# Seven weight slots, three natural expert pairs and one wide ordered pair in the middle of a two-layer backbone step

## The reference

```
def hier_moe(h, w_group, b_group, w_expert, b_expert, w_gate, w_up, w_down):
    ...
    g_prob = jax.nn.softmax(xf @ w_group + b_group, axis=-1)
    p_grp, g_idx = lax.top_k(g_prob, 1)
    ...
    e_w, e_idx = lax.top_k(jax.nn.softmax(e_logit, axis=-1), TOP_K_INNER)
    ...
    act = jax.nn.silu(jnp.einsum('td,edf->tef', x, w_gate)) * jnp.einsum('td,edf->tef', x, w_up)
    act = act * combine[..., None]
    y = jnp.einsum('tef,efd->td', act, w_down)
```

## Time and profile before

| | us |
|---|---|
| median of 3 timed runs | 1143.74 (1143.3 to 1143.93) |
| profiled execution | 1141.77 |
| its span | 1139.6 |
| PE busy | 981.8 (86%) |
| VectorE busy | 291.4 (26%) |
| ScalarE busy | 195.5 (17%) |
| GpSimd busy | 24.8 (2%) |

### The profile page before, as it was taken

How to read it: one execution, slowest core, us unless ns; L and a number is a source line. 1 busy time by engine, 2 the same in 40 slices (tenths; PEclk the granted TensorE clock), 3 DMA queues, 4 the chain that set the end, 5 groups by cost and what they waited for, 6 DMA issues and landing times.

```text
span 1139.6 us, 13423 instructions
## 1 busy us (share of the span) xinstructions
PE 981.8 (86%) x5665; PEld 528.6 (46%) x5665; DVE 291.4 (26%) x644; ACT 195.5 (17%) x348; POOL 24.8 (2%) x45
## 2 busy tenths in 40 slices
PE   3799999989899786886699999999997998968873
PEld 1475454454466444552244444444444654535541
DVE  1310236722642111110402222231006312111103
ACT  1111122250311000010112122353003110000001
POOL 2000000000000000000000011000000000000000
PEclk9999999989899998998889999999998899989987
DMA  9999729983169999999954444046341499999992
GB/s 303 395 348 370 301 84 391 409 343 119 53 237 366 415 416 418 415 416 416 387 187 148 155 152 182 28 148 239 148 153 68 173 368 416 419 416 414 417 417 97
DMA packets 77794, 323.28 MB, mean 284 GB/s; under 512 B 4892, under 2 KB 4948, under 8 KB 61092
## 3 DMA queue, kind: packets, MB, share of 16 engines
q1 hardware_dynamic: 74756, 312.78, 69.7%
q0 software_dynamic: 2976, 9.61, 2.4%
HBM read 316.34 MB, written 6.03 MB: 283 GB/s over the span
## 4 chain that ended last, share of the span: by engine, by line
PE 65%; DMA 21%; DVE 6%; SPq 4%; ACT 2%; issue 2%; DVEq 0%
PE PS L595 62%; DMA ring<-in_moe_w_gate 11%; DMA ring<-in_moe_w_down 8%; SPq L502 3%; DMA ring<-in_mod_w 2%; DVE H L1519 1%; DVE scratch L1509 1%; PE PS L641 1%; SPq L469 1%; ACT L1199 0%; DVE scratch L1544 0%; DVE X L1546 0%; ACT scratch L1197 0%; SPq L488 0%; DVE scratch L1723 0%
## 5 line engine op out<-in xcount | busy, mean ns | idle before, releaser
L595 PE MATMUL PS<-ring,scratch 128*32 128x256 f32 (+4 forms) x2720 | 306.8, 464 | 83.0 <-DMA ring<-in_moe_w_gate 35.2
L595 PEld LDWEIGHTS PS<-ring,scratch 128*32 128x32 f32 (+2 forms) x2720 | 150.9, 128 | 236.8 <-issue 201.4
L595 PE MATMUL PS<-ring,HT 128*128 128x512 f32 x576 | 253.5, 596 | 3.8 <-issue 2.7
L595 PEld LDWEIGHTS PS<-ring,HT 128*128 128x128 f32 x576 | 108.7, 191 | 135.5 <-issue 132.6
L595 PE MATMUL PS<-scratch 128*128 128x512 f32 (+2 forms) x440 | 117.1, 437 | 4.4 <-issue 1.5
L595 PEld LDWEIGHTS PS<-scratch 128*128 128x128 f32 (+1 forms) x440 | 56.0, 193 | 59.9 <-issue 55.8
L595 PE MATMUL PS<-scratch,H 128*128 128x128 f32 x640 | 82.4, 284 | 0.0
L1922 DVE TENSOR_TENSOR scratch<-PS,scratch 128x256 f32<-128x256 f32 x20 | 8.5, 425 | 287.4 <-ACT scratch L1350 287.4
L595 PEld LDWEIGHTS PS<-scratch,H 128*128 128x128 f32 x640 | 77.3, 198 | 9.2 <-issue 9.2
L595 PE MATMUL PS<-ring,cpad 128*32 128x512 f32 x384 | 46.9, 628 | 14.0 <-DMA ring<-in_mod_w 14.0
L1350 ACT ACTIVATE scratch<-PS 128x256 f32<-128x256 f32 x20 | 7.7, 384 | 268.5 <-PE PS L595 268.5
(11 more groups left out here) (272 smaller groups left out, 620.0 us busy)
## 6 DMA issues: line engine op xcount, KB each, us to landing
ring<-in_moe_w_gate SPq DMA_DIRECT2D x56, 1024.0 KB, 18.2
ring<-in_moe_w_up SPq DMA_DIRECT2D x56, 1024.0 KB, 20.5
ring<-in_moe_w_down SPq DMA_DIRECT2D x56, 1024.0 KB, 19.3
ring<-in_mod_w SPq DMA_DIRECT2D x24, 2048.0 KB, 16.6
ring<-in_odd_w_in SPq DMA_DIRECT2D x12, 2048.0 KB, 14.0
ring<-in_even_w_in SPq DMA_DIRECT2D x7, 2048.0 KB, 15.3
ring<-in_moe_w_gate SPq DMA_DIRECT2D x4, 2048.0 KB, 15.0
ring<-in_moe_w_up SPq DMA_DIRECT2D x4, 2048.0 KB, 12.9
```

The source lines that it names most:

```text
L595: return nc.tensor.matmul(out, lhsT, rhs, start=start, stop=stop, skip_group_check=True, **kw)
```

## The change

- RING goes from 6 to 7. The space comes from the descriptor scratch of GpSimd's transfers, set to 2048 bytes in each partition, and from CKV, which loses its own tile.
- CKV moves into the second half of `gain`, beside GNA. Its two loads go from the start of GpSimd's program behind GNA's load, and `next_gain(1)` goes behind the two attention outputs and waits in addition for `attn_out_done` to reach 2, when the cached values have been read.
- NFIX goes from 4 to 6 and NWIDE from 4 to 2; TILES puts three natural pairs first and one ranked wide pair at place 6, with three narrow tiles on each side.
- The semaphore `count_ready` goes; who read CNT behind it now waits for `who_ready`, and VectorE waits for CNT's write itself.

```diff
-NFIX = 4
+NFIX = 6
 NRANK = NE - NFIX
-NWIDE = 4
-TILES = [2, 2, 4, 4, 2, 4, 4, 2, 4, 4]
+NWIDE = 2
+TILES = [2, 2, 2, 4, 4, 4, 2, 4, 4, 4]
...
-RING = 6
+RING = 7
...
-        CKV = sb("CKV", [P, 2, 2 * P])
+        CKV = gain[:, 512:1024].rearrange("p (a n) -> p a n", a=2)
...
-        count_ready = sem("count_ready")
...
-                sp.wait_ge(count_ready, l + 1)
+                sp.wait_ge(who_ready, l + 1)
...
-            pool.dma_start(CKV[:, 0, :], A["cache_attn_k"][0, 0].rearrange("t h d -> t (h d)")).then_inc(late_params_in, 16)
-            pool.dma_start(CKV[:, 1, :], A["cache_attn_v"][0, 0].rearrange("t h d -> t (h d)")).then_inc(late_params_in, 16)
...
             pool.dma_start(GNA, A["hgrn_norm_g"][0].rearrange("h v -> (h v)").partition_broadcast(P))\
                 .then_inc(late_params_in, 16)
+            pool.dma_start(CKV[:, 0, :], A["cache_attn_k"][0, 0].rearrange("t h d -> t (h d)")).then_inc(late_params_in, 16)
+            pool.dma_start(CKV[:, 1, :], A["cache_attn_v"][0, 0].rearrange("t h d -> t (h d)")).then_inc(late_params_in, 16)
...
-            pool.wait_ge(gs_ready, 1)
-            next_gain(1, A["norm2_g"][0])
-
             pool.wait_ge(attn_qk_ready, 1)
...
+            pool.wait_ge(gs_ready, 1)
+            pool.wait_ge(attn_out_done, 2)
+            next_gain(1, A["norm2_g"][0])
             pool.wait_ge(out_sem, 32)
...
-                    V.tensor_scalar(CNT[:, 0:1], s1[:, 22:23], 0.0, None, ALU.max).then_inc(count_ready, 1)
+                    st.link(V.tensor_scalar(CNT[:, 0:1], s1[:, 22:23], 0.0, None, ALU.max))
...
-    nc = bacc.Bacc("TRN2", target_bir_lowering=False, num_devices=1)
+    nc = bacc.Bacc("TRN2", target_bir_lowering=False, num_devices=1, dynamic_dma_scratch_size=2048)
```

More of the change, by code:

```diff
@@ L1044, in moe @@
                 scatter(1)
-                pe.wait_ge(count_ready, l + 1)
+                pe.wait_ge(who_ready, l + 1)
                 most = pe.value_load(CNT[0:1, 0:1], min_val=0, max_val=S * P)
@@ L1366, in moe @@
                     tile(t)
-                act.wait_ge(count_ready, l + 1)
+                act.wait_ge(who_ready, l + 1)
                 most = act.value_load(CNT[0:1, 0:1], min_val=0, max_val=S * P)
@@ L1949, in moe @@
                     tile(t)
-                dve.wait_ge(count_ready, l + 1)
+                dve.wait_ge(who_ready, l + 1)
                 most = dve.value_load(CNT[0:1, 0:1], min_val=0, max_val=S * P)
```

## The result

The changed kernel took 1137.38 us (median of 5, 1136.46 to 1138.41) beside 1143.3 us of the kernel before (median of 5, 1142.44 to 1143.93): a ratio of 0.9948 [0.9934, 0.9963], 5.9 us faster. The profiled executions are closer together: 1137.52 for 1141.77, spans 1135.3 for 1139.6, 4.3 us.

The account below looks back on a forecast made before the run. Expert blocks were taken as bound by the DMA's restart plus loads left, the start by load bytes. Gains 0.6 + 1.5 + 1.5 = 3.6 us off the median 1143.74 gave 1140.1 us, range 1137.5 to 1143.2.

Parts of the forecast that it names:

- The entry of the expert block: Each expert block: third wide tile starts DMA's full run 18.6 us later, 4 loads (20.1 us) fewer left; gain 1.5 us.
- The seventh slot filled in time: Load ring ahead of the expert block: the seventh load is natural, needs no ranking, and is issued at about 281 us.
- rival C: Expert blocks: seventh slot not full at block start, 3.5 us lost in each, 1150.1 us in all; chance 0.09.
- Rival A: Expert blocks: third wide tile doesn't hold the DMA up, slot saves 5.03 us twice, 1133.0 us in all; chance 0.10.
- Rival B: Expert blocks: wide tile eats the slot's gain, 0.3 to 1.0 us remain in each, 1141.1 to 1142.5; chance 0.23.
- The start: Program start: two 128 KB loads of cached keys and values leave GpSimd's queue, 0.6 us gained, bounds 0 to 1.3.
- The moved norm gain and the scratch: After attention, GpSimd's queue: later gain load has 15 us of cover, worth nothing; smaller scratch 0, up to 1 us above.
- the last step of the sum: Whole run: the profiled execution was 2.0 us under the timed median 1143.74; the 3.6 us gain is taken off the median.

Follow-up runs that it names:

- the first experiment: The changed kernel with the tiles of before (two natural pairs, four ranked wide experts), seven slots kept: 1131.73 us, 0.9907 of the kernel before.

## Why the prediction was right or wrong

**The entry of the expert block: right.** The full run starts at the load that the third tile's down projection frees, 370.4 us (forecast 371.3 less the 0.6 of the start), with no gap behind it; and PE waits for no load in the first three tiles. The blocks got 1.73 and 1.65 us shorter, for a forecast of 1.5 and bounds of 1.0 to 2.2. Tiles and slot alone gave +3.3 and −5.1, where the forecast's figures make 18.6 − 15.1 = 3.5 and 5.03. The 2 us between an issue and the DMA's start were worked out loosely (0.44 of the stretch before 356 us puts the start at 354.2, so 1.5 us), but they stand in both restarts and cancel.

**The seventh slot filled in time: right**, at 280.27 us, so rival C is out; the kernel of six slots with the new tiles shows what it would have cost, 3.3 and 3.4 us in the blocks.

**Rival A: wrong for this change**, right for the slot with the old tiles. The rule that I weighed there, from the Trainium skill (Perfetto Trace Analysis, Optimization Strategy), is that a repeated gap can mean too little room for the next tile, by the count of buffers or the size of tiles. The trace agrees that another buffer closes the gap (0.44 to 1.04 in the first experiment). The gap that the wide third tile opens again (0.52) stands with the same seven slots of the same size: PE frees three of them there in the time in which a narrow tile frees six.

**Rival B: wrong.** The third tile didn't end late, and the DMA ran at 424 GB/s in the first full stretch and at 413 to 418 in the slices, not at 428 throughout; the blocks gained 1.65 and more, for 0.3 to 1.0.

**The start: agrees, not shown.** PE's fourth weight block comes 37.73 − 36.88 = 0.85 us earlier and everything to the first projection with it, for a forecast of 0.6. Single executions scatter by as much. The nine profiles without idle matmuls make 0.6 on average, the four with them point the other way, and the times of the run with only the rest of the change don't decide.

**The moved norm gain and the scratch: nothing, as said.** GpSimd and VectorE of the changed kernel in order of time (before: the earlier trace rows):

```profile
48.98 0.77 POOL L555 DMA_DIRECT2D scratch<-in_state_hgrn  x1
...
57.20 0.76 POOL L555 DMA_DIRECT2D scratch<-in_state_hgrn  x1 [7.46 <-issue]
...
245.53 0.54 POOL L545 DMA_DIRECT2D gain<-in_norm_g  x1 [33.18 <-issue]
...
266.61 2.35 DVE L1498 SCALAR_TENSOR_TENSOR scratch<-PS,gain 128x1024 f32<-128x1024 f32 x2 [27.80 <-PE PS L594]
```

The gain is loaded at 245.53, its reader waits for PE until 266.61 and for nothing else.

**Between the blocks: not foreseen, and it cancels.** The last down projection of block 0 takes 0.83 us longer than the earlier trace rows showed; the turn before the second block takes 1.44 us less, of which 0.93 is left at that block's start (below).

**What failed is the last step of the sum, "the difference goes off the median".** The terms were made against the profiled execution of 1141.77, and I carried them to a median of three, 1143.74, taking the 2.0 us between the two for something that belongs to before and stays. It doesn't: before's median was 1142.3, 1141.87 and 1142.94 in 21, 19 and 17 runs, 0.1 to 1.2 us over the profiled execution, so that execution was an ordinary one and the three runs were high. Nor does the changed kernel show such a difference: its profiled execution took 1137.52, its median is 1137.38. From the profiled execution the same 3.6 us give 1138.2, 0.8 over the result. So of the 2.7 us between 1140.1 and 1137.38 this step makes 2.0; 0.65 are the terms' shortfall (4.25 us in the two profiles for 3.6). The range allowed for the bounds of the terms, 1138.0 to 1142.7, and 0.5 us on either side; medians of few runs of this kernel differ by 1 to 2 us. That the time lies below the range by as little as 0.12 us is chance: the changed kernel's repetition, 1138.09, lies within it. How much of the first comparison's 5.9 us is the change can be told from the repetitions: 3.8 and 3.1 us between medians of more runs, 4.3 between the profiles. Why before's first runs were high stays open.

## What to carry to other kernels

In this kernel a buffer more in the ring was worth its whole transfer only where the consumer freed the earlier ones at the old pace. Where the tiles at the ring's entry are changed too, follow the loads one by one and ask which release starts the run that never stops again. Change one of ring and tile order at a time: here the two had opposite signs, and the slot alone gained 10.6 us where both together gained 3.1 to 5.9. Take a forecast off an anchor of many runs, or widen the range by what medians of few runs differ.

## What the runs showed of the hardware that I had not expected

The granted clock decides a few stretches of a program that looks bound by loads. The turn of PE before the second block, the kernel before and then the changed one:

```profile
883.77 6.65 PE L595 MATMUL PS<-scratch,H 128*128 128x128 f32 x32
```

```profile
882.54 5.21 PE L594 MATMUL PS<-scratch,H 128*128 128x128 f32 x32
```

The stretch of 4 us in them, before and then after:

```profile
884.00:888.00 4.00, 4.00 (x20) 4.00 (x21) 2.09 (x8) 0.41 (x1) 0.00 (x0) 0.50 0.00 0
```

```profile
884.00:888.00 4.00, 3.97 (x29) 3.73 (x28) 0.77 (x5) 0.60 (x1) 0.00 (x0) 0.82 0.00 0
```

The same 32 matmuls take 1.4 us less where the mean clock is 0.82 for 0.50. The last down projection of block 0, which begins behind 5.2 us without work, goes the other way: 5.66 before, 6.49 us after. Without idle matmuls all four profiles with six slots read like before here and all five with seven like after. With idle matmuls at the start, almost 500 us earlier, the two kernels change places: 6.29 and then 5.17 us in the kernel before, 5.39 and 6.58 in the changed one. So slots and tiles as such don't decide it; what sets the moment at which the level returns wasn't tried.

In the kernel before, GpSimd issued the two loads of initial states in one go:

```profile
48.77 1.51 POOL L556 DMA_DIRECT2D scratch<-in_state_hgrn  x2
```

After the change, with two more loads ahead of them and the descriptor scratch of 2048 bytes, the second went at 57.20 us behind 7.46 us that no semaphore explains (GpSimd's rows beside the moved norm gain, further up). With four more loads at the start both went at 57.55 us, behind 6.51 us. Whether the loads ahead or the scratch causes it wasn't tried, since every run has both or neither. Nothing waited for that load here; a queue with less slack might pay.
